# Gate products of three column quarters as seven products per pair of token tiles, with the loads that have to move

## The reference

```python
proj = x @ w_in
glu_in, q, k, v, q_mem, gate_logits = jnp.split(proj, split_points(), axis=-1)
y_conv = conformer_conv(...)          # (S, 512) @ w_conv_out -> (S, 1024)
y_attn = windowed_gqa(...) @ w_attn_out
y_mem = memory_attention(...) @ w_mem_out
gates = jax.nn.sigmoid(gate_logits + b_gate).reshape(B, S, N_BRANCHES, D)
merged = gates[:, :, 0] * y_conv + gates[:, :, 1] * y_attn + gates[:, :, 2] * y_mem
x = layer_norm(DEEPNORM_ALPHA * x + merged @ w_o, ln1_g, ln1_b)
gate, up = jnp.split(x @ w_ffn_in, 2, axis=-1)
ffn = (jax.nn.silu(gate) * up) @ w_ffn_out
return layer_norm(DEEPNORM_ALPHA * x + ffn, ln2_g, ln2_b)
```

## Time and profile before

| what | value |
|---|---|
| median of the runs shown | 989.97 us (988.91 to 991.08, 3 runs) |
| profiled execution | 989.88 us |
| its span, slowest core | 988.8 us |
| spans of the eight cores | 984.0 to 988.8 us |
| TensorE busy | 951.9 us, 96% |
| VectorE, ScalarE, GpSimd busy | 547.9, 407.6, 286.7 us |

### The profile page before, as it was taken

The page is one execution under the profiler, slowest core; times in us unless marked ns, Lnnn a source line. Parts: engine busy times, 40 slices in busy tenths (PEclk is TensorE's granted clock), DMA queues, the critical chain, the costliest instruction groups (busy, mean ns, idle before and its releaser), DMA issues.

```text
span 988.8 us, 16315 instructions; the slowest of 8 cores (984.0 to 988.8 us)
## 1 busy us (share of the span) xinstructions
PE 951.9 (96%) x5530; PEld 449.7 (45%) x5628; DVE 547.9 (55%) x908; ACT 407.6 (41%) x655; POOL 286.7 (29%) x296
## 2 busy tenths in 40 slices
PE   4999999999999999999999999999999999999997
PEld 1455545444444444444445444444444444444444
DVE  1324475666773222223468679976475676663565
ACT  1135667575662222222244456655222344443211
POOL 3200000212144334333321244534333233333331
PEclk9999999999999999999999999999999999999999
DMA  8997034564239999921067176655533323220222
GB/s 125 173 176 146 24 90 107 72 122 85 46 65 140 139 144 141 151 63 66 1 187 281 33 171 171 171 142 127 169 128 127 107 86 107 87 86 1 86 107 86
DMA packets 39538, 112.12 MB, mean 113 GB/s; under 512 B 4960, under 2 KB 16872, under 8 KB 38336
## 3 DMA queue, kind: packets, MB, share of 16 engines
q0 software_dynamic: 11104, 41.16, 28.4%
q1 hardware_dynamic: 28352, 69.91, 22.2%
HBM read 132.49 MB, written 30.47 MB: 165 GB/s over the span
## 4 chain that ended last, share of the span: by engine, by line
PE 86%; DMA 4%; DVE 3%; issue 3%; ACT 3%; POOL 0%; DVEq 0%; SPq 0%; ACTq 0%; POOLq 0%
PE ps L233 84%; DMA arena<-xt 2%; DMA arena<-w_bf_cache 2%; ACT arena L597 1%; ACT arena L645 1%; PE ps L1107 1%; DVE arena L1164 1%; DVE arena L1043 1%; DVE arena L1039 1%; POOL arena L147 0%; DVE arena L590 0%; DVE arena L805 0%; ACT arena L600 0%; PE ps L760 0%; PE ps L688 0%
## 5 line engine op out<-in xcount | busy, mean ns | idle before, releaser
L233 PE MATMUL ps<-arena 128*128 128x512 bf16 (+4 forms) x5120 | 934.3, 358 | 28.3 <-DMA arena<-xt 15.2
L233 PEld LDWEIGHTS ps<-arena 128*128 128x128 bf16 (+2 forms) x5218 | 429.7, 98 | 517.2 <-issue 61.9
L836 DVE SCALAR_TENSOR_TENSOR arena<-arena,ps 128x512 f32<-128x512 f32 x96 | 65.9, 687 | 145.6 <-PE ps L233 141.3
L815 ACT ACTIVATE arena<-ps,bgate_sb 128x512 f32<-128x512 f32 x96 | 65.9, 687 | 164.8 <-PE ps L233 164.8
L1161 ACT COPY arena<-ps 128x512 f32<-128x512 f32 x132 | 76.6, 585 | 137.4 <-PE ps L233 137.4
L1171 POOL TENSOR_TENSOR arena<-arena 128x512 bf16<-128x512 f32 x66 | 88.6, 1343 | 150.6 <-DVE arena L1164 150.5
L1164 DVE TENSOR_TENSOR arena<-arena,ps 128x512 f32<-128x512 f32 x132 | 88.1, 684 | 40.3 <-PE ps L233 39.8
L843 POOL TENSOR_TENSOR arena<-arena 128x512 f32<-128x512 f32 x32 | 40.7, 1273 | 123.8 <-DVE arena L836 123.8
L1021 ACT ACTIVATE arena<-arena 128x1024 bf16<-128x1024 f32 x31 | 32.7, 1056 | 85.1 <-DVE arena L1320 73.9
L147 POOL DMA_DIRECT2D arena<-w_g x21 | 11.3, 546 | 167.9 <-PE ps L233 166.7
L1043 DVE SCALAR_TENSOR_TENSOR arena<-arena,rs 128x1024 bf16<-128x1024 f32 (+2 forms) x33 | 56.6, 1717 | 1.8 <-DVE arena L1039 0.3
(11 more groups left out here) (111 smaller groups left out, 449.7 us busy)
## 6 DMA issues: line engine op xcount, KB each, us to landing
arena<-w_bf_cache SPq DMA_DIRECT2D x44, 512.0 KB, 3.6
arena<-u_scratch SPq DMA_DIRECT2D x64, 135.0 KB, 3.2
arena<-x SPq DMA_DIRECT2D x16, 512.0 KB, 10.6
y_scratch<-arena SPq DMA_DIRECT2D x16, 512.0 KB, 3.3
arena<-y_scratch SPq DMA_DIRECT2D x16, 512.0 KB, 3.5
out<-arena SPq DMA_DIRECT2D x15, 512.0 KB, 2.6
arena<-w_f POOLq DMA_DIRECT2D x22, 256.0 KB, 4.5
arena<-w_g POOLq DMA_DIRECT2D x9, 512.0 KB, 20.3
```

The costliest lines, as they stand in the source:

```text
L233: return pe.run(lambda: nc.tensor.matmul(out, lhsT, rhs, start=start, stop=stop, skip_group_check=onto), deps, inc)
L815: t = act.run(lambda: nc.scalar.activation(gb[r], ps[:, bk, :], AF.Tanh, bias=bgate[:, b * 8 + dc:b * 8 + dc + 1], scale=0.5), [tk, gb_fre ...
L836: t_y = dve.run(lambda: nc.vector.scalar_tensor_tensor(out=gb[r], in0=gb[r], scalar=1.0, in1=ps[:, bk, :], op0=ALU.add, op1=ALU.mult), [tk ...
```

## The change

Quarters 1 to 3 of the gate stage are computed unit by unit (`c_unit`): a quarter, a pair of token tiles Q and a branch. The gate's 1024 input channels and 256 columns are split in two halves each, the tokens in two tiles, and the four results come from seven products of four matmuls (with sums of weight blocks, `fold_wg`, and of token blocks, `token_sums`) in place of eight. The sixteen branch matmuls of the unit stand between the products. The partial results are copied out of PSUM by ScalarE and completed by VectorE; the fourth gate is finished in the next unit. The second token tile of each pair is overwritten by one of the sums. The token sums of the first pair and the first fold are placed in the last items of quarter 0 (`sums_now`), the others in the units of quarter 1; each fold stands one unit ahead of its use.

The sums take memory, and so loads move. The output weights go from the end of quarter 1 to the middle of quarter 3. Of the x rows, 0 and 1 go to the middle of quarter 3 and row 2 to its end. The LN1 table, one transfer at the start of quarter 1, becomes two: its first row at the end of quarter 2, its second behind the gate stage, ahead of x rows 3 to 15. W1's group 2 is loaded behind those x rows, and its fold stands behind the second block's addition in the output projection. The gate weights have a new order in DRAM (four blocks per branch), and the gates of quarter 0 read it through `WSLOT`. The diff, cut to its core:

```diff
-    w_g_d = din("w_g", [128, 4, 3, 8, 256])
+    w_g_d = din("w_g", [128, 4, 3, 4, 4, 128])
...
-    def fold(buf, dep):
-        G = buf.rearrange("p s k c -> p s (k c)")
-        t1 = dve.run(lambda: nc.vector.tensor_tensor(out=G[:, 4:6, :], in0=G[:, 1:3, :], in1=G[:, 0:2, :], op=ALU.subtract), [dep])
-        t2 = dve.run(lambda: nc.vector.tensor_tensor(out=G[:, 6, :], in0=G[:, 2, :], in1=G[:, 4, :], op=ALU.subtract), [t1])
-        return dve.run(lambda: nc.vector.tensor_tensor(out=G[:, 1, :], in0=G[:, 3, :], in1=G[:, 6, :], op=ALU.subtract), [t2])
+    def fold(raw, sums, dep):
+        B, S = (a.rearrange("p s k c -> p s (k c)") for a in (raw, sums))
+        t1 = dve.run(lambda: nc.vector.tensor_tensor(out=S[:, 0:2, :], in0=B[:, 1:3, :], in1=B[:, 0:2, :], op=ALU.subtract), [dep])
+        t2 = dve.run(lambda: nc.vector.tensor_tensor(out=S[:, 2, :], in0=B[:, 2, :], in1=S[:, 0, :], op=ALU.subtract), [t1])
+        return dve.run(lambda: nc.vector.tensor_tensor(out=B[:, 1, :], in0=B[:, 3, :], in1=S[:, 2, :], op=ALU.subtract), [t2])
+
+    def halves(P, A):
+        return [A[:, P, i, 4 * j:4 * j + 4, :] for i in range(2) for j in range(2)]
+
+    def token_sums(A, S, deps):
+        A11, A12, A21, A22 = A
+        tok = [None] * 5
+
+        def sub(i, out, a, b, need, op=ALU.subtract):
+            f = "p k t -> p (k t)"
+            tok[i] = dve.run(lambda: nc.vector.tensor_tensor(
+                out=out.rearrange(f), in0=a.rearrange(f), in1=b.rearrange(f), op=op), need)
+
+        return tok, [lambda: sub(1, S[:, 0], A21, A22, deps, ALU.add),
+                     lambda: sub(2, S[:, 1], S[:, 0], A11, [tok[1]]),
+                     lambda: sub(3, A21, A11, A21, [tok[1]]),
+                     lambda: sub(4, S[:, 2], A12, S[:, 1], [tok[2]])]
...
-        bk, tk = group8(lambda kc: wg[:, b, kc, dci * 128:(dci + 1) * 128], lambda kc: xT[:, tt, kc, :], tt, [t_wg[dp, b]])
+        bk, tk = group8(lambda kc: wg[:, b, WSLOT[kc // 4][dci], kc % 4, :], lambda kc: xT[:, tt, kc, :], tt, [t_wg[dp, b]])
...
+    SG = [V(140.5, [128, 3, 4, 512]), V(156.5, [128, 3, 4, 512])]
+    WS = {(dp, b): V(o, [128, 3, 4, 128]) for dp, at in ((1, (152.5, 172.5, 193.75)), (2, (152.5, 172.5, 193.75)), (3, (48, 172.5, 51)))
+          for b, o in enumerate(at)}
...
+    def fold_wg(dp, b, deps):
+        t_ws[dp, b] = fold(wgs[dp % 2][:, b], WS[dp, b], [t_wg[dp, b], deps])
+
+    def c_unit(dp, Q, b, work):
+        raw, sums, wo = wgs[dp % 2][:, b], WS[dp, b], wos[dp % 2]
+        A11, A12, S3, A22 = halves(Q, xh)
+        S1, S2, S4 = (SG[Q][:, i] for i in range(3))
+        sa = sg_tok[Q]
...
+        def product(bk, form, rhs, first, deps):
+            for kc in range(4):
+                w = raw[:, form, kc, :] if form < 4 else sums[:, form - 4, kc, :]
+                tk = mm(ps[:, bk, :], w, rhs[:, kc, :], first and kc == 0, kc == 3,
+                        deps if kc == 0 else (), inc=(kc == 3), onto=not first)
+            return tk
...
+        def copy(bk, tk):
+            buf, free = tiles.pop(0)
+            return buf, act.run(lambda: nc.scalar.copy(buf, ps[:, bk, :]), [tk, free])
+
+        def plus(buf, bk, deps):
+            return dve.run(lambda: nc.vector.tensor_tensor(out=buf, in0=buf, in1=ps[:, bk, :], op=ALU.add), deps)
...
+        def gated(i, j, buf, t_th, o):
+            bk, tk = o
+            t_y = dve.run(lambda: nc.vector.scalar_tensor_tensor(
+                out=buf, in0=buf, scalar=1.0, in1=ps[:, bk, :], op0=ALU.add, op1=ALU.mult), [tk, t_th])
+            banks.release(bk, t_y)
...
+            t = pool.run(lambda: nc.gpsimd.tensor_tensor(out=out, in0=acc, in1=buf, op=ALU.add), [t_acc, t_y])
+            tiles.append((buf, [t]))
...
+        x, dx = banks.alloc(1)
+        k11, t1 = copy(x, product(x, 0, A11, True, [dx, t_wg[dp, b], t_xt[2 * Q:2 * Q + 2]]))
+        last = [f() for f in c_pend[:1]]
+        y, dy = banks.alloc(1)
+        t_c = plus(k11, y, [product(y, 3, A12, True, [dy]), t1])
+        banks.release(y, t_c)
+        for f in c_pend[1:]:
+            f(*last)
+        del c_pend[:]
+        th11 = tanh(k11, k11, 0, [t_c])
+        o11 = branch(0, 0)
+        k12, t_u = copy(x, product(x, 6, S2, False, [t1, t_ws[dp, b], sa[2]]))
+        z, dz = banks.alloc(1)
+        t5 = product(z, 4, S1, True, [dz, sa[1]])
+        o22 = branch(1, 1)
+        gated(0, 0, k11, th11, o11)
+        for f in work:
+            f()
+        k22, t3 = copy(x, product(x, 5, S3, False, [t_u, sa[3]]))
+        t_c22 = plus(k22, z, [t5, t3])
+        th22 = tanh(k22, k22, 1, [t_c22])
+        gated(1, 1, k22, th22, o22)
+        o21 = branch(1, 0)
+        o12 = branch(0, 1)
+        k21, free = tiles.pop(0)
+        th21 = tanh(k21, ps[:, x, :], 0, [product(x, 1, A22, False, [t3]), free])
+        banks.release(x, th21)
+        t_p = product(z, 2, S4, False, [t_c22, sa[4]])
+        t_c12 = plus(k12, z, [t_p, t_u])
+        banks.release(z, t_c12)
+        gated(1, 0, k21, th21, o21)
+        c_pend.append(lambda: tanh(k12, k12, 1, [t_c12]))
+        c_pend.append(lambda th: gated(0, 1, k12, th, o12))
+        return t_p
...
+    for at, fn in ((-12, lambda: sums_now(0)), (-9, lambda: sums_now(1)), (-6, lambda: fold_wg(1, 0, [sg_tok[0][1]])), (-3, lambda: sums_now(2))):
+        mains[at] = behind(mains[at], fn)
...
-    X1 = [V(o, [128, D], F32) for o in (156.5, 160.5, 164.5, 172.5)] + [V(68 + 4 * i, [128, D], F32) for i in range(12)]
+    X1 = [V(o, [128, D], F32) for o in (8, 12, 156.5, 160.5)] + [V(68 + 4 * i, [128, D], F32) for i in range(12)]
...
-    t_ln1 = load(ln1t, bass.AP(ln1_d.tensor, 0, [[0, 128], [D, 2], [1, D]]), [a_done, t_sT[3, 3]], sp)
     load_wg(2, [pe.tok()])
     cache_w1(4)
-    straight(cat([c_main(1, tt) for tt in range(4)]))
-    load_wg(3, [pe.tok()])
-    t_wo = load(w_o_sb, w_o_d, [a_done])
-    cache_w1(3)
-    straight(cat([c_main(2, tt) for tt in range(4)]))
+
+    def load_ln1(i, deps):
+        t_ln1[i] = load(ln1t[:, i, :], bass.AP(ln1_d.tensor, D * i, [[0, 128], [1, D]]), deps, sp)
+
+    sums_begin(1, [a_done])
+    for dp in (1, 2):
+        for Q in range(2):
+            for b in range(3):
+                u_done = pe.tok()
+                work = []
+                if Q == 0 and b < 2:
+                    work.append(lambda: fold_wg(dp, b + 1, [u_done, s_done]))
+                if Q == 1 and b == 2:
+                    work.append(lambda: fold_wg(dp + 1, 0, [u_done]))
+                if dp == 1 and Q == 0:
+                    work += (sg_steps[0][3:], sg_steps[1][0:2], sg_steps[1][2:])[b]
+                c_unit(dp, Q, b, work)
+        if dp == 1:
+            load_wg(3, [pe.tok()])
+            cache_w1(3)
...
-    w1_free = [[dp2_done], [dp2_done, gb_free[0]], [dp2_done, gb_free[1]], []]
+    w1_free = [[dp2_done], [dp2_done, gb_free[0]], [], []]
...
-    for u in range(3):
+    load_ln1(0, [dp2_done])
+    for u in range(2):
         load_w1(u)
-    for tb in range(3):
-        load_x(tb, [dp2_done])
-    straight(c_main(3, 0))
-    for u in range(3):
-        straight(c_main(3, u + 1))
-        fold_w1(u)
+    for b in range(3):
+        u_done = pe.tok()
+        c_unit(3, 0, b, [lambda: fold_wg(3, b + 1, [u_done])] if b < 2 else [])
+    q0_done = pe.tok()
+    t_wo = load(w_o_sb, w_o_d, [q0_done])
+    for tb in range(2):
+        load_x(tb, [q0_done])
+    for b in range(3):
+        c_unit(3, 1, b, [lambda: fold_w1(b)] if b < 2 else [])
+    c_flush()
     c_done = pe.tok()
-    g_done = t_mg[3, 3, 1]
+    g_done = t_mg[3, 2, 1]
+    w1_free[2] = [c_done, g_done]
     w1_free[3] = [c_done, g_done]
-    for tb in (3, *range(4, 16)):
+    load_x(2, [c_done])
+    load_ln1(1, [c_done, g_done])
+    for tb in range(3, 16):
         load_x(tb, [c_done, g_done])
-    load_w1(3)
+    for u in (2, 3):
+        load_w1(u)
...
             e_sums(0, [c_done] + [x1_free[i] for i in range(4)])
         d_H(tb)
+        if tb == 1:
+            fold_w1(2)
         if 1 <= tb <= 12:
```

More of the change, by code:

```diff
@@ L778, in _build @@
     merged = [V(54, [128, 2, T]), V(116.5, [128, 2, T]), V(124.5, [128, 2, T]), V(132.5, [128, 2, T])]
[L779 removed]
+    wgs = [V(o, [128, 3, 4, 4, 128]) for o in (32, 175.75)]
     wos = [V(48, [128, 3, 4, 256]), V(187.75, [128, 3, 4, 256])]
@@ L859, in c_main, with sums_begin @@
         return out
+    xh = xT.rearrange("p (q i) k t -> p q i k t", q=2)
+    SG = [V(140.5, [128, 3, 4, 512]), V(156.5, [128, 3, 4, 512])]
+    sg_tok, sg_steps = [None, None], [None, None]
+    WS = {(dp, b): V(o, [128, 3, 4, 128]) for dp, at in ((1, (152.5, 172.5, 193.75)), (2, (152.5, 172.5, 193.75)), (3, (48, 172.5, 51)))
+          for b, o in enumerate(at)}
+    t_ws = {}
+    tiles = []
+    c_pend = []
+    def sums_begin(Q, deps):
+        sg_tok[Q], sg_steps[Q] = token_sums(halves(Q, xh), SG[Q], deps)
@@ new lines, in fold_wg, with branch, tanh @@
+    def fold_wg(dp, b, deps):
[11 more added lines that the diff above has]
+            return tk
+        def branch(i, j):
```

(47 more changed lines are left out.)

21 lines of the change are left out of this document (16 added, 5 removed).

## The result

The changed kernel takes 997.14 us (median) against 989.97: a ratio of 1.0071, 95% interval 1.0055 to 1.0087. It is slower by 0.7%. The profiled execution took 997.14 us; the span of its slowest core is 996.1 against 988.8.

What follows compares the result with a forecast made beforehand. TensorE's matmul count was taken to bound the kernel. From 989.88 us: -15.5 (matmuls) + 2 (unit waits) + 18.5 (wait before the transposes) + 2 (backlog and clock) = +7.0, forecast 997, range 988 to 1006.

Steps and rivals of the forecast that it cites:

- backlog and clock: Behind the transposes' wait: VectorE work left over for TensorE to wait on, and a lowered clock; together 2 us, between 1.1 and 4.
- The matmuls saved: Gate stage, quarters 1 to 3: 18 units each issue 44 matmuls instead of 48, 72 fewer, saving 15.5 us.
- what the units wait: Gate stage: TensorE loses 2 us to VectorE's folds and token sums, bounds 0 and 6.
- the upper bound of 6 us: Gate stage: TensorE's loss if all token sums and half the folds meet GpSimd additions.
- The spare time of 3.6 us per unit: Gate stage: VectorE's free time between the first gated product and the addition the seventh product needs, 3.6 us.
- The W1 landing: Behind the gate stage: W1 group 2, fifteenth in its queue, lands at t0 + 32.5.
- TensorE's wait: Output projection, before the first transposes: TensorE stands still 18.5 us for VectorE's scaling, queued behind the late W1 fold.
- t0: The end of the last gate-stage matmul, 498.9 in the kernel before; later times are counted from it.
- The wait of block 7 on block 5's addition: Output projection, after the first transposes: TensorE waits for VectorE's late addition, about 1.1 us.
- The output weights: Issued mid-quarter 3, 28.5 us before t0; even landing at t0 + 6, they would cost nothing inside the later wait.
- That W1 would not wait for the x rows: Rival, SP queue behind the gate stage: W1 group 2 lands early; about 984, or 976.5 if by t0 + 14; chance 0.14.
- That VectorE becomes the bound of the gate stage: Rival: GpSimd additions stretch VectorE's two-input operations; stage loss about 12 in place of 2, time 1007; chance 0.12.

## Why the prediction was right

The time was forecast at 997.0 and measured at 997.14. The mechanism is the one forecast, and each term agrees to about 1 us. That the sum agrees to 0.1 us is luck: TensorE's idle time ahead of the transposes came out 0.5 us above what was taken, backlog and clock 0.7 below.

**The matmuls saved, less what the units wait.** -15.5 + 2 = -13.5; the stage is 13.6 shorter. The wait of 1.3 us fell in the second unit, the one that has a fold and two sums, where 0.8 to 1.7 was worked out. Seven of the ten folds in these units met a GpSimd addition, more than the half that the upper bound of 6 us was reckoned with, and no other unit waited. The spare time of 3.6 us per unit is measured too: with the load moved ahead, VectorE does this in that unit:

```profile
327.21 0.68 DVE L806 TENSOR_TENSOR arena<-arena 128x1024 bf16<-128x1024 bf16 x1
...
328.00 1.30 DVE L807 TENSOR_TENSOR arena<-arena 128x512 bf16<-128x512 bf16 x1
...
329.40 0.43 DVE L808 TENSOR_TENSOR arena<-arena 128x512 bf16<-128x512 bf16 x1
...
329.75 2.55 DVE L819 TENSOR_TENSOR arena<-arena 128x2048 bf16<-128x2048 bf16 x2
...
332.21 0.68 DVE L923 TENSOR_TENSOR arena<-arena,ps 128x512 f32<-128x512 f32 x1
```

From 327.21 to 332.21 it works 5.0 us on fold and sums, and TensorE loses 1.3: 3.7 us were free.

**The W1 landing and TensorE's wait.** t0 + 32.5 was worked out, t0 + 33.2 measured: the queue opened at t0 + 4.1 in place of 4.4, its first transfer took 6.6 us in place of 5.1, and fourteen more took 1.61 each in place of 1.64. The wait is 18.0 in place of 18.5. The gap of 1.07 us ahead of the first block, which I had not foreseen, is hidden in it: without the gap, the six blocks would end earlier and the wait be longer by as much. So TensorE's idle time there is 19.0 in all. The fold's place in VectorE's order (the kernel with the fold later), its load's place in the queue (the two kernels with the load moved) and the size per place in the queue are each shown by a run.

**Backlog and clock.** 2 was taken, 1.3 measured: from the transposes to the end 996.1 - 525.6 = 470.5 us against 988.8 - 519.6 = 469.2. By the window from 525 to 530 (busy for 4.43 us at 0.52) the clock alone cost about 2.1. Against it stand small waits in the channel projection and behind it, 0.9 us in sum where the kernel before had 1.6. The wait of block 7 on block 5's addition did not show. That VectorE caught up while TensorE ran at 1.2 GHz is the likely reason, but it is not shown.

**The output weights** landed 16.1 us after their issue at 459.92, 9.6 us ahead of t0: no wait, as argued.

```profile
arena<-w_o POOLq DMA_DIRECT2D x1, 2048.0 KB, 16.1
```

**The rivals.** That W1 would not wait for the x rows is refuted by the landing in the changed kernel and by its moving with the place in the queue: for these transfers landing kept the order of issue, and what the Trainium skill says on completion (DMA: Bandwidth & Descriptors, "Queues, rings and completion order"), that it is not first-in first-out for an issuing engine, did not come to bear. That VectorE becomes the bound of the gate stage is refuted by the stage's length; but the rule on VectorE and GpSimd (the Trainium skill, SBUF — State Buffer, "Practical consequences"), that two such instructions exclude each other, is borne out by single operations: the executions of line 807 that took 1.30 us or more are the ones beside a GpSimd addition. The kernels with extra sums show where it would have decided: two sums per unit cost 17.6 us, more than the stage gained.

What stays open is why the slowest core did not follow when the gap ahead of the output projection was shortened.

## What to carry to other kernels

When work is added to a kernel and a load has to move for want of memory, follow the load to the instruction that waits for it, and that instruction's place in its engine's order: one fold that stood 24 us ahead of its data cost more than 72 matmuls gave. Price it as issue time plus place in the queue times the time per transfer, and then count what stands behind the waiting instruction until TensorE needs it. If the sum is bad, sending the one load ahead, or moving the waiting instruction behind the work that has its data, costs one line: here 19.5 us, 2% of the program.
